# Moving one token sum, one weight correction, one tile pair and one copy's semaphore in a nine-stage fp32 transformer kernel

## The reference, cut to what matters

```
def conv_glu_ffn(h, w_up, conv_w, conv_b, w_down):
    S = h.shape[1]
    a, b = jnp.split(h @ w_up, 2, axis=-1)
    a_pad = jnp.pad(a, ((0, 0), (CONV_WIDTH_2 - 1, 0), (0, 0)))
    a = sum(conv_w[j] * a_pad[:, j:j + S] for j in range(CONV_WIDTH_2)) + conv_b
    return (jax.nn.silu(a) * b) @ w_down
...
def second_block(...):
    cos32, sin32 = rope_tables(positions, A_QK_DIM // ROPE_FRAC)
    cos16, sin16 = rope_tables(positions, B_HEAD_DIM // ROPE_FRAC)
...
    for i in range(DEPTH_2):
...
        mem_o = memory_cross_attention(q_mem, mem_n, w_mem_kv[i])
        x = x + jnp.concatenate([mix, mem_o], axis=-1) @ w_out
        x = x + conv_glu_ffn(rmsnorm(x, g_ffn[i]), f_w_up[i], f_conv_w[i], f_conv_b[i], f_w_down[i])
    return rmsnorm(x, g_final)
```

## Time and profile before

| | us |
|---|---|
| median of 3 runs | 2069.52 (2067.0 to 2071.22) |
| profiled execution, its own time | 2067.44 |
| its span in the profile | 2065.7 |
| PE busy | 2034.7 (99%) |
| DVE busy | 1207.0 (58%) |
| POOL busy | 1021.0 (49%) |
| ACT busy | 939.8 (45%) |

### The profile page before, as it was taken

The page is one execution under the profiler, slowest core; times in us unless marked ns, Lnnn a source line. Parts: engine busy times, 40 slices in busy tenths (PEclk is TensorE's granted clock), DMA queues, the critical chain, the costliest instruction groups (busy, mean ns, idle before and its releaser), DMA issues.

```text
span 2065.7 us, 30139 instructions
## 1 busy us (share of the span) xinstructions
PE 2034.7 (99%) x11590; PEld 1744.7 (84%) x11590; DVE 1207.0 (58%) x2215; ACT 939.8 (45%) x1525; POOL 1021.0 (49%) x483
## 2 busy tenths in 40 slices
PE   9999999999999999999999999999999999999998
PEld 6888977888898989876877898989887688989997
DVE  4889788673642433477985463646423936645563
ACT  3345545354442334534366542434432956434343
POOL 3433432434575757442623575757344036665663
PEclk9999999999999999999999999999999999999999
DMA  9654322234233333332211433333433034333422
GB/s 371 241 182 143 103 62 62 88 102 163 76 108 92 103 113 93 104 108 70 80 24 52 128 102 94 101 113 92 143 97 74 2 85 114 103 102 102 123 72 92
DMA packets 282551, 220.91 MB, mean 107 GB/s; under 512 B 13521, under 2 KB 266577, under 8 KB 280113
## 3 DMA queue, kind: packets, MB, share of 16 engines
q1 hardware_dynamic: 271712, 195.75, 31.1%
q10 hardware_dynamic: 10704, 23.33, 3.7%
HBM read 213.56 MB, written 2.10 MB: 104 GB/s over the span
## 4 chain that ended last, share of the span: by engine, by line
PE 85%; DVE 8%; ACT 2%; issue 2%; POOL 1%; DMA 0%; ACTq 0%; DVEq 0%; SPq 0%; POOLq 0%
PE bank L1047 59%; PE bank L1126 12%; PE bank L1346 2%; PE bank L1537 2%; PE bank L1559 2%; DVE arena L3098 1%; PE bank L1494 1%; DVE small L3096 1%; PE bank L1546 1%; PE bank L1647 1%; PE bank L1394 1%; POOL w_split L3286 1%; DVE bank L2575 1%; PE bank L1405 1%; DVE entry_sum L2893 1%
## 5 line engine op out<-in xcount | busy, mean ns | idle before, releaser
L1047 PE MATMUL bank<-h_hi,w_split 128*128 128x512 f32 x2832 | 865.1, 382 | 2.0 <-POOL w_split L3286 1.1
L3286 POOL TENSOR_TENSOR w_split<-wslots,w_split 128x2048 fp32r<-128x2048 f32 (+3 forms) x119 | 471.0, 3960 | 638.3 <-ACT w_split L1801 626.7
L1047 PEld LDWEIGHTS bank<-h_hi,w_split 128*128 128x128 f32 x2832 | 534.7, 189 | 93.0 <-issue 16.2
L1047 PE MATMUL bank<-h_lo,w_split 128*128 128x512 f32 x1416 | 537.5, 380 | 0.0
L1801 ACT ACTIVATE w_split<-wslots 128x2048 fp32r<-128x2048 f32 (+2 forms) x114 | 194.0, 1702 | 359.1 <-PE bank L1047 308.9
L1047 PE MATMUL bank<-hid_hi,w_split 128*128 128x512 f32 x1056 | 316.6, 379 | 1.3 <-POOL w_split L3330 0.9
L1047 PEld LDWEIGHTS bank<-h_lo,w_split 128*128 128x128 f32 x1416 | 267.8, 189 | 38.7 <-issue 3.4
L1047 PEld LDWEIGHTS bank<-hid_hi,w_split 128*128 128x128 f32 x1056 | 199.6, 189 | 31.0 <-issue 1.6
L1047 PE MATMUL bank<-hid_lo,w_split 128*128 128x512 f32 x528 | 200.1, 379 | 0.0
L3319 POOL TENSOR_TENSOR entry<-entry_sum,entry 128x512 fp32r<-128x512 f32 x108 | 155.8, 1470 | 71.8 <-ACT entry L2127 71.8
L2575 DVE SCALAR_TENSOR_TENSOR bank<-arena,cols,bank 128x512 f32<-128x512 f32 x240 | 161.2, 749 | 5.4 <-ACT bank L1915 4.9
(11 more groups left out here) (376 smaller groups left out, 3163.1 us busy)
## 6 DMA issues: line engine op xcount, KB each, us to landing
wslots<-in_f_w_up SPq DMA_DIRECT2D x88, 512.0 KB, 4.9
wslots<-in_w_in SPq DMA_DIRECT2D x24, 1024.0 KB, 5.3
wslots<-in_w_ffn_up SPq DMA_DIRECT2D x44, 512.0 KB, 4.7
arena<-in_w_ada ACTq DMA_DIRECT2D x8, 2048.0 KB, 9.8
wslots<-in_a_w_in SPq DMA_DIRECT2D x10, 1024.0 KB, 5.2
arena<-in_w_ada_first SPq DMA_DIRECT2D x8, 1024.0 KB, 18.5
wslots<-in_f_w_down SPq DMA_DIRECT2D x8, 1024.0 KB, 5.1
wslots<-in_f_w_down SPq DMA_DIRECT2D x16, 512.0 KB, 3.9
```

The lines of the kernel that those rows point to most:

```text
L1047: return nc.tensor.matmul(bank[:], w, woven(x), start=start, stop=stop)
L3286: last = nc.gpsimd.tensor_tensor(part[:, 1, cols_of], slot(p, 1, size)[:, 0, cols_of], part[:, 0, cols_of].bitcast(F32), ALU.subtract)
```

## The change

Four edits. (1) For `k = 1, 2` VectorE makes the three weight sums for unit (0, 2) before the fourth token sum, and ScalarE casts that token sum's upper part after the unit's seven upper parts. (2) On GpSimd, for all three `k`, the lower part of token sum 1 stands after the lower parts of weight entries 0 and 1, so third. (3) VectorE makes two angle tables, merges tile pair 0, and then makes the other two tables. (4) The first two key copies count on `mem_in` and the last two on `dup_ready`; TensorE waits for the first two ahead of the scores, and for the others in the eighth group, ahead of the ninth. The semaphore counts follow; the two pieces of the diff that only count (in `lower_counts` and `sum_counts`) are left out below.

```
@@ -145,6 +145,8 @@
                         did(k, part, i + 1, e)
+                    if k and (part, i) == (0, 1):
+                        did(k, "token_sum", 3)
                 if i == part == 0 and k in SEVEN:
@@ -152,7 +154,7 @@
                     did(k, part, i + 1, "first")
-                if i == part == 0 and k in SEVEN:
+                if i == part == 0 == k and k in SEVEN:
                     did(k, "token_sum", 3)
@@ -1112,10 +1115,10 @@
                     if e < 6:
-                        pe.wait_ge(S["sums_lower"], LOWER[unit] + e + 1)
+                        pe.wait_ge(S["sums_lower"], LOWER[unit] + e + 1 + (e > 1 and unit[1:] == (0, 2)))
                     else:
                         if unit[1:] == (0, 2):
-                            pe.wait_ge(S["sums_lower"], LOWER[unit] + 7)
+                            pe.wait_ge(S["sums_lower"], LOWER[unit] + 8)
                         pe.wait_ge(lo_ready[q], SPLITS_BEFORE[FIRST[name] + 2 * i] + 1)
@@ -1743,11 +1746,11 @@
             pe.wait_ge(*emptied("b_v", 0))
-            pe.wait_ge(S["dup_ready"], 16 * 5)
+            pe.wait_ge(S["mem_in"], 16 * 3)
             pe.wait_ge(S["rope_ready"], 28)
...
             attend(2, b_fill, {0: lambda: mem_queries(2 * DT - 3), 1: lambda: mem_queries(2 * DT - 2), 2: lambda: mem_queries(2 * DT - 1),
-                               SUM_LAG: lambda: wait_emptied(pe, "b_qmem")})
+                               SUM_LAG: lambda: wait_emptied(pe, "b_qmem"), 2 * TB - 1: lambda: pe.wait_ge(S["dup_ready"], 16 * 3)})
             output("b_out", 2, b_fill)
@@ -2122,7 +2125,7 @@
 
-                for e, made in enumerate((1, 3, 4, 4)):
+                for e, made in enumerate((1, 3, 5, 5) if k and (part, i) == (0, 2) else (1, 3, 4, 4)):
                     act.wait_ge(S["angle_then_sum_ready"], SUMS[k, part, i] + made)
@@ -2141,7 +2144,7 @@
 
-                act.wait_ge(S["angle_then_sum_ready"], SUMS[k] + (4 if j == 3 else 3))
+                act.wait_ge(S["angle_then_sum_ready"], SUMS[k] + ((7 if k else 4) if j == 3 else 3))
                 nc.scalar.activation(token_sums[j][0][:], token_plain[j], ACT.Copy).then_inc(S["softplus_then_sums_upper"], 1)
@@ -2196,6 +2199,8 @@
                             block_uppers(*following)
+                            if k and following[1:] == (0, 2):
+                                token_upper(k, 3)
                         else:
@@ -2223,7 +2228,7 @@
                         gate_and_upper(2 * i + 1, p, following)
-                        if first_pair:
+                        if first_pair and not k:
                             token_upper(k, 3)
@@ -2479,7 +2484,7 @@
                 for half in (0, 64):
-                    act.dma_start(kw_heads[half:half + 64, head // 64:4:2, :], key_tiles[head:head + 64, :, :]).then_inc(S["dup_ready"], 16)
+                    act.dma_start(kw_heads[half:half + 64, head // 64:4:2, :], key_tiles[head:head + 64, :, :]).then_inc(S["dup_ready" if head else "mem_in"], 16)
             for b in range(TB):
@@ -2760,7 +2765,8 @@
             steps.settle()
-            for k in range(4):
+            def angles(k):
+
                 width, quarter = "32" if k < 2 else "64", 0.25 if k % 2 == 0 else 0.0
@@ -2777,7 +2783,8 @@
 
-            for j in range(4):
+            def mixed(j):
+
                 p, use = one("conv_pw", j)
@@ -2806,6 +2813,14 @@
 
+            for k in range(2):
+                angles(k)
+            mixed(0)
+            for k in range(2, 4):
+                angles(k)
+            for j in range(1, 4):
+                mixed(j)
+
             def residual(name, tiles, gate=None, norm=None):
@@ -2948,6 +2963,8 @@
                         three_sums(*following)
+                        if following == (k, 0, 2) and k:
+                            last_token_sum(k)
                         if unit:
@@ -2958,8 +2975,6 @@
                     turn(2 * i + 1, (lambda: early_sums(*following)) if following else None)
-                    if i == part == 0 < k and k in SEVEN:
-                        last_token_sum(k)
 
@@ -3304,13 +3319,15 @@
                 if j == 1:
-                    pool.wait_ge(S["angle_then_sum_ready"], SUMS[k] + 4)
+                    pool.wait_ge(S["angle_then_sum_ready"], SUMS[k] + (7 if k else 4))
                 nc.gpsimd.tensor_tensor(token_sums[j][1][:], token_plain[j], token_sums[j][0][:].bitcast(F32), ALU.subtract).then_inc(S["sums_lower"], 1)
...
                 for e, block in enumerate((None, None, None, None, (0, 0), (0, 1), (1, 1))):
+                    if (part, i, e) == (0, 2, 2):
+                        token_lower(k, 1)
                     hi, lo = entries[k][e]
@@ -3353,8 +3370,6 @@
                         if seven_at(k, part, i):
-                            if part == 0 and i == 2:
-                                token_lower(k, 1)
                             entry_lowers(k, part, i)
```

More of the change, by code:

```diff
@@ L171, in lower_counts @@
                     if seven_at(k, part, i):
-                        n += i == 2 and part == 0
                         at[k, part, i] = n
-                        n += 7 if i == 2 and part == 0 else 6
+                        n += 8 if i == 2 and part == 0 else 6
         n += 1
@@ L187, in sum_counts @@
         at[k] = n
-        n += 4
+        n += 3 if k else 4
         for part, (_, tiles) in enumerate(PARTS):
@@ L193, in sum_counts @@
                     n += 4
+                    if k and part == 0 and i == 1:
+                        n += 1
                 if seven_at(k, part, i) and k == 0:
```

20 lines of the change are left out of this document (9 added, 11 removed).

## The result

| | before | after |
|---|---|---|
| median, us | 2069.52 (2067.0 to 2071.22) | 2059.04 (2058.34 to 2059.94) |
| profiled execution, its own time | 2067.44 | 2058.34 |
| its span | 2065.7 | 2056.5 |

The ratio is 0.995, with a 95% interval of 0.9938 to 0.9961: faster by 8.1 to 12.8 us. The forecast was 2060.9 us, 8.65 less than before.

What follows compares the result with a forecast made beforehand. TensorE, busy for 99% of the span, was taken to bound the kernel, so only its instructions or waits count. The terms -6.5 - 1.95 - 0.2 = -8.65 against the median 2069.52 gave 2060.9 us, range 2057.5 to 2064.5.

Steps and rivals of the forecast that it cites:

- Edit 3, 6.5 us: Pointwise convolution, job 2: TensorE's 4.84 us bank wait and 1.67 us of low clock go; 4.8 if the low clock stays.
- The margin of 0.2 us at the spread: Root's spread: the inverse ends at 471.04, TensorE asks for it at 471.25.
- The cast behind the sines: ScalarE's next weight cast starts at 473.96; cast and lower part end at 480.54, 2.0 us ahead of need.
- Edit 4, 1.95 us: Last attention's scores: the first two key copies land before the queries end, so TensorE's wait vanishes; bounds 0 and -1.96.
- the 0.1 that I gave as a sign of being right: Last attention: scores start within 0.1 us of the last query if the forecast is right.
- Edits 1 and 2, 0.2 us: Feed-forwards 1 and 2: each 0.64 us wait ahead of the seven products becomes 0.5; both places -0.2, bounds -1.3 and +1.4.
- T: Feed-forward 1: end of VectorE's fourth weight sum, 1199.67 before; forecast 1198.5, between 1197.2 and 1199.3.
- The spread: Rival at the root's spread: VectorE's and ScalarE's chain 2 us late, up to 2 us lost, 2063; chance 0.08.
- The copies: Rival at the scores: the second key copy lands with the fourth, so no gain there, 2062.9; chance 0.06.
- The waits at the units: Rival in feed-forwards 1 and 2: GpSimd does not hold the sums and the waits vanish, 2059.8; chance 0.07.
- The slower case: Rival in two feed-forwards: ScalarE's conversion 6.1 us later, 7.8 us lost in each, 2076.6; chance 0.03.
- No change: Rival for the whole kernel: something beside TensorE paces it and the lead is given back, 2069.5; chance 0.04.

Runs made afterwards that it cites:

- one_table: The changed kernel with tile pair 0 merged behind one angle table instead of two: 2065.2 us, ratio 0.9981.
- tables_only: The kernel before with only the merge of tile pair 0 moved between the angle tables: 2062.2 us, ratio 0.9968.
- tables_again: The same kernel as `tables_only`, profiled once more: 2064.76 us.
- part_first: The changed kernel with GpSimd making the lower part of token sum 1 ahead of the weight entries again: 2059.68 us, ratio 0.9956.
- upper_late: The changed kernel with the fourth token sum's upper part on ScalarE moved from ahead of the conversion to behind it: 2057.59 us, ratio 0.9945.

## Why the prediction was right, step by step

- **What bounds.** Right: TensorE stayed at 99%, and the lead changed only at waits and low-clock stretches of TensorE.
- **Edit 3, 6.5 us.** Right in both halves: 6.56 in the first trace and in every other one that has it, of which 0.06 to 0.10 go again at the spread. The 1.67 us of low clock went with the wait. Its size was that of one execution: by the four traces above, the low clock costs 1.7 to 2.8 us. The low bound of 4.8 needed a low stretch without its wait, which no trace showed at job 2. The margin of 0.2 us at the spread was real and about 0.1; `one_table` shows what lies beyond it. The cast behind the sines was the next late thing but hurt nobody, as counted: it starts at 473.79, and its lower part ends at 480.35, 2 us ahead of need.
- **Edit 4, 1.95 us.** Right in mechanism, 0.39 too much in the first trace: 0.40 us of wait stayed, not the 0.1 that I gave as a sign of being right, and the step was 1.56; in the other traces with it 1.82 to 2.03. I had taken the second copy's landing from a mean of two, which put it 0.6 us ahead of the queries' end. The second copy took 6.97 us from issue to landing in the trace before and 7.94 in the one after. The ninth group has no wait, as counted. One premise was read from too little: the clock was 1.00 right behind this wait in the first profile, but in `tables_only` and `tables_again` the same wait drew a low stretch of 1.54 us. The 1.95 is the wait's worth where no such stretch follows.
- **Edits 1 and 2, 0.2 us.** Right, and 0.32 by the lead (0.15 and 0.17). The token sum's upper part, 1.0 us in front of the conversion, ate most of the earlier weight sum. After the change T is 1191.32 (1189.56 + 1.76), with the lead of 7.3 us 1198.6 against the 1198.5 that I chose. That it came so near is in part luck: 1198.5 was the middle between two bounds. The rows of the kernel after (DVE twice, ACT, PE), which answer to the earlier trace rows:

```profile
1187.33 2.30 DVE L2904 TENSOR_TENSOR token_half<-token_half 128x1024 f32<-128x1024 f32 x1
1189.56 1.76 DVE L2908 TENSOR_TENSOR entry_sum<-wslots,entry_sum 128x512 f32<-128x512 f32 x1
...
1194.92 0.76 ACT L2177 ACTIVATE arena<-bank,cols 128x512 f32<-128x512 f32 x1
...
1200.18 2.05 PE L1129 MATMUL bank<-token_sum,entry 128*128 128x256 f32 x16 [0.49 <-DVEq L2880]
```

  The token sum is held (2.30 us against 1.22), and so is the fourth weight sum (1.76 against 0.69). Together that is 2.15 us of hold, where I had put 1.9. GpSimd's new order was counted at nothing; `part_first` has it at 0.28 us a place. In feed-forward 0 it costs nothing, as counted: the lead is 6.63 at 490 us and 6.66 at 1040. The bounds for a vanished wait were too small: by `upper_late` it is worth 0.9 us a place, not 0.64.
- **The sum.** 8.65 forecast. The four touched places give 6.56 + 1.56 + 0.15 + 0.17 = 8.44 in the first trace; 0.58 more came from a low stretch in the first attention that this trace lacks, and that is luck. The medians differ by 10.5, with an interval that begins at 8.1, so the 1.8 us beyond my sum are not shown to be real. Part of it has a source in the traces: I took job 2's low clock from an execution in which it was short, and over the four traces with that wait it costs 0.4 us more in the mean. That the change also saves chance low stretches at the scores would fit, but two in five traces with the wait against two in nine without do not settle it: this stays open.
- **The rivals.** The spread did not take the wait, by 0.1 us. The copies gained, in every trace with edit 4. The waits at the units stayed, at 0.5 us. The slower case did not come near: the conversion was 0.15 us earlier, not 6.1 later. No change is ruled out by the interval.

## What to carry to other kernels

Where one engine is busy for 99% of the span, read the list of its waits and follow what each released: two tables moved behind one merge gave more than the 4.84 us that the wait's row shows, because the low clock behind that wait went with it. Ask of each moved step which queue it lands in: the same 1.0 us cast was free while ScalarE stood and cost nearly all of edit 1's gain in front of the critical conversion; two lines further down it was free again. And compare traces by the n-th instruction of the bounding engine: steps of 0.16 us are plain there, where the intervals of the medians here reach about 2 us to either side. Take more than one trace of a kernel, though: what the low clock costs at one place differs by 1 us and more between executions.

## What the runs showed of the hardware that I had not expected

- In the attention stages a stretch at the lower clock stands in some executions and not in others, of one and the same kernel: at the same wait of 2.25 us in 5 of 14 traces (0.6 to 1.5 us lost), behind the same wait of 1.8 to 2.0 us in 2 of 5 (1.54 us). In two traces it stands where no wait in the stage passed 0.92 us (1.52 and 1.47 us lost).
- The low stretch behind one and the same wait of 4.8 us differs: 12.12 us from job 2 to the spread in two traces, 12.74 and 13.25 in two others. Behind the 3.9 us wait it lasted 6.7 us and cost 3.35.
- Four equal copies of 256 KB from one queue land in 6.6, 7.0, 7.3 and 8.0 us in the trace before; the second of them takes 7.2 to 7.9 us in the seven traces with edit 4 and uncut copies, against 6.9 to 7.1 in the five without. Why is open.
